# A decoder trunk: eight gate units move into the RG-LRU stage and eight w_rg units into the stick-breaking pairs

## The reference

```
proj = h @ w_in      # RG-LRU x | RG-LRU gelu gate | stick-breaking qkv | FoX qkv | forget logits | 3 merge gates
xa = causal_depthwise_conv(rg_x, conv_w, conv_b)
ya = gelu(rg_gate) * rg_lru(xa, ...)                 # r, i from block-diagonal products, then a scan over tokens
yb = merge_heads(stick_breaking_attention(q_b, k_b, v_b))        # 8 heads x 64
yc = merge_heads(forgetting_attention(q_c, k_c, v_c, log_f))     # 8 heads x 64
g = sigmoid(merge + merge_b).reshape(bsz, slen, 3, 1024)
mixed = g[:, :, 0] * (ya @ w_rg) + g[:, :, 1] * (yb @ w_sb) + g[:, :, 2] * (yc @ w_fox)
return mixed @ w_o
```

## Time and profile before

| what | value |
|---|---|
| median of three runs | 2886.98 us (2884.0 to 2891.76) |
| the profiled execution: its time | 2893.89 us |
| its span, first to last instruction | 2892.1 us |
| PE busy | 2730.0 us (94%), 13124 matmuls |
| DVE, ACT, POOL busy | 1219.5, 1059.9, 1176.4 us |
| mean granted TensorE clock | 0.977 of full speed |

### The profile page before, as it was taken

The page is one execution under the profiler, slowest core; times in us unless marked ns, Lnnn a source line. Parts: engine busy times, 40 slices in busy tenths (PEclk is TensorE's granted clock), DMA queues, the critical chain, the costliest instruction groups (busy, mean ns, idle before and its releaser), DMA issues.

```text
span 2892.1 us, 35341 instructions
## 1 busy us (share of the span) xinstructions
PE 2730.0 (94%) x13124; PEld 2272.7 (79%) x13124; DVE 1219.5 (42%) x1608; ACT 1059.9 (37%) x1593; POOL 1176.4 (41%) x471
## 2 busy tenths in 40 slices
PE   3999998899999999999989999988999999999998
PEld 3888886687788888888888888767777888788886
DVE  6655337855421134511145553577545111444111
ACT  4222236554432234222242222565444322432223
POOL 2555433422234444544435554333221444355443
PEclk9999998999999999999999999989999999999999
DMA  5555531211123333533335555211111333244333
GB/s 213 205 203 190 168 123 59 73 45 44 52 74 96 100 96 111 175 101 102 93 128 200 186 196 160 89 59 53 50 52 44 95 94 96 74 175 142 92 102 95
DMA packets 91303, 325.73 MB, mean 113 GB/s; under 512 B 10097, under 2 KB 12529, under 8 KB 90865
## 3 DMA queue, kind: packets, MB, share of 16 engines
q1 hardware_dynamic: 91120, 323.35, 34.2%
HBM read 321.21 MB, written 2.10 MB: 112 GB/s over the span
## 4 chain that ended last, share of the span: by engine, by line
issue 54%; POOL 33%; PE 12%; POOLq 0%; ACT 0%; DVE 0%; ACTq 0%; DVEq 0%
POOL w_lo L383 32%; PE bank L1143 4%; PE bank L1142 4%; PE bank L1141 4%; POOL wab_lo L389 1%; POOLq L381 0%; ACT fin L729 0%; POOL tmp L366 0%; DVE fin L1134 0%; DVE x L792 0%; ACTq L93 0%; PE bank L1198 0%; ACT rstd L426 0%; ACT tmp L418 0%; ACT rstd L423 0%
## 5 line engine op out<-in xcount | busy, mean ns | idle before, releaser
L383 POOL TENSOR_TENSOR w_lo<-raw,w_hi 128x1024 fp32r<-128x1024 f32 x443 | 1157.5, 2622 | 1565.1 <-ACT w_hi L412 1564.7
L1141 PE MATMUL bank<-h_hi,w_hi 128*128 128x512 f32 x2240 | 883.9, 395 | 0.5
L1142 PE MATMUL bank<-h_lo,w_hi 128*128 128x512 f32 x2240 | 877.8, 392 | 0.0
L1143 PE MATMUL bank<-h_hi,w_lo 128*128 128x512 f32 x2240 | 876.8, 391 | 0.0
L412 ACT ACTIVATE w_hi<-raw 128x1024 fp32r<-128x1024 f32 x443 | 468.1, 1057 | 1010.9 <-PE bank L1143 933.9
L1141 PEld LDWEIGHTS bank<-h_hi,w_hi 128*128 128x128 f32 x2240 | 425.3, 190 | 89.7 <-POOL w_lo L383 1.3
L1143 PEld LDWEIGHTS bank<-h_hi,w_lo 128*128 128x128 f32 x2240 | 424.2, 189 | 89.8
L1142 PEld LDWEIGHTS bank<-h_lo,w_hi 128*128 128x128 f32 x2240 | 425.1, 190 | 87.6
L740 DVE CUSTOM_DVE_ANT_0 ada<-ada,c_act 128x1024 f32<-128x1024 f32 x144 | 255.2, 1779 | 265.3 <-DMA ada<-ada_w 265.1
L1143 PE MATMUL bank<-g_hi,w_lo 128*128 128x512 f32 (+1 forms) x792 | 295.2, 373 | 0.0
L1142 PE MATMUL bank<-g_lo,w_hi 128*128 128x512 f32 (+1 forms) x792 | 292.4, 369 | 0.0
(11 more groups left out here) (200 smaller groups left out, 3055.5 us busy)
## 6 DMA issues: line engine op xcount, KB each, us to landing
raw<-w_units SPq DMA_DIRECT2D x443, 512.0 KB, 3.6
ada<-ada_w SPq DMA_DIRECT2D x144, 512.0 KB, 4.5
ada<-ada_w SPq DMA_DIRECT2D x8, 1024.0 KB, 16.5
x<-x_in SPq DMA_DIRECT2D x4, 512.0 KB, 7.3
wab_raw<-wab SPq DMA_DIRECT2D x2, 1024.0 KB, 5.8
y<-fin SPq DMA_DIRECT2D x8, 256.0 KB, 2.2
c_act<-c_rows SPq DMA_DIRECT2D x1, 512.0 KB, 3.7
vec<-vecs SPq DMA_DIRECT2D x3, 92.5 KB, 3.3
```

Source lines behind the costliest of these rows:

```text
L383: nc.gpsimd.tensor_tensor(w_lo[s][:, :, :], raw[u % RAW][:, :, :], w_hi[s][:, :, :].bitcast(F32), ALU.subtract).then_inc(unit_lo.sem, 1)
L1141: nc.tensor.matmul(o, wh, xh, start=start, stop=False, skip_group_check=True)
L1142: nc.tensor.matmul(o, wh, xl, start=False, stop=False, skip_group_check=True)
L1143: return nc.tensor.matmul(o, wl, xh, start=False, stop=stop, skip_group_check=True)
```

## The change

The first merge gate's eight units (`gate0`, from `h`) now stand in the RG-LRU stage: one in front of each `gates(c)`. Their sigmoids go into a new buffer `part`. The eight w_rg units (`w_rg`, from `ya`) stand in the stick-breaking pairs, two in each: one behind `scores`, one between the next pair's k and v units, both into bank 7. DVE multiplies each into `part` (`first_part`). The merge has three units for each block instead of five and alternates between two sets of banks. The units are numbered and stored in the new order. Because `ya` is used up when the FoX pairs begin, the FoX outputs lie in its memory (`yf_hi`, `yf_lo`), the stick-breaking outputs in `ys_hi`, `ys_lo`; several small buffers of the RG-LRU stage have other addresses. All instructions that compute remain; none is added but in another form (each block's product with the first gate goes into `part` in place of `mx`).

The core of the diff: numbering and memory, then ACT, DVE and PE:

```
+def U_X(c):
+    return U_RG + 6 * (c // 2) + 2 * (c % 2)
+
+
+def U_GATE0(n):
+    return U_RG + 6 * (n // 2) + 4 + n % 2
+
+
+def U_Q(p, j):
+    if p == 0:
+        return U_QKV + j
+    if p <= 4:
+        return U_QKV + 3 + 5 * (p - 1) + (1, 2, 4)[j]
+    return U_QKV + 23 + 3 * (p - 5) + j
+
+
+def U_WRG(n):
+    return U_QKV + 3 + 5 * (n // 2) + (0, 3)[n % 2]
 
 
...
+        yf_hi = at("yf_hi", 0, [P, 4, T], F32R)
+        yf_lo = at("yf_lo", 8192, [P, 4, T], F32R)
+        ys_hi = at("ys_hi", 32768, [P, 4, T], F32R)
+        ys_lo = at("ys_lo", 40960, [P, 4, T], F32R)
+        part = at("part", 49152, [P, KD, T])
+
...
-                tick(l, U_RG + 2 * c0 + 4)
+                tick(l, U_GATE0(c0))
                 nc.scalar.preload_act_table_set("sigmoid_and_others")
                 for c in both:
                     s, b = c % 2, 4 + 2 * (c % 2)
+                    act.wait_ge(unit_done.sem, unit_done.at(l, U_GATE0(c) + 1))
+                    A(part[:, c, :], bank[2 * s + 1][:, :], ACT.Sigmoid,
+                      bias=vec[:, V_MERGEB + c:V_MERGEB + c + 1]).then_inc(sg0_ready.sem, 1)
+                    tick(l, U_GATE0(c) + 1)
...
-                u = U_QKV + 3 * p
+                u = U_Q(p, 0)
+                if 1 <= p <= 4:
+                    tick(l, u - 1)
                 if p:
                     tick(l, u)
...
+            def first_part(l, n):
+
+                if n == 0:
+                    dve.wait_ge(sg0_ready.sem, sg0_ready.at(l, KD))
+                dve.wait_ge(unit_done.sem, unit_done.at(l, U_WRG(n) + 1))
+                V.tensor_tensor(part[:, n, :], part[:, n, :], bank[7][:, :], ALU.mult).then_inc(part_ready.sem, 1)
+
...
+                sg = [tmp[2 * (n % 2) + g] for g in range(2)]
+                dve.wait_ge(sg_ready.sem, sg_ready.at(l, 2 * n + 2))
+                dve.wait_ge(unit_done.sem, unit_done.at(l, U_TAIL + 3 * n + 3))
+                if n == 0:
+                    dve.wait_ge(part_ready.sem, part_ready.at(l, KD))
+                for g in range(2):
+                    V.tensor_tensor(sg[g][:, :], sg[g][:, :], bank[4 + 2 * (n % 2) + g][:, :],
+                                    ALU.mult).then_inc(mx_step.sem, 1)
+                for g in range(2):
+                    dve.wait_ge(mx_step.sem, mx_step.at(l, 4 * n + (1, 3)[g]))
+                    V.tensor_tensor(part[:, n, :], part[:, n, :], sg[g][:, :], ALU.add).then_inc(mx_step.sem, 1)
...
+                for p in range(4):
+                    sb_softplus(l, p, 0)
+                    first_part(l, 2 * p)
+                    sb_softplus(l, p, 1)
+                    q_rest(l, p + 1)
+                    v_rest(l, p)
+                    sb_split(l, p, 0)
+                    sb_split(l, p, 1)
+                    k_rest(l, p + 1)
+                    first_part(l, 2 * p + 1)
+                    y_rest(l, p)
+                for p in range(4, PAIRS):
...
+                    if p < 4:
+                        pe.wait_ge(part_ready.sem, part_ready.at(l, 2 * p + 2))
...
                 pe.wait_ge(vt_ready.sem, vt_ready.at(l, p + 1))
-                if p:
+                if p < 4:
+                    pe.wait_ge(part_ready.sem, part_ready.at(l, 2 * p + 1))
+                else:
...
+            def gate0(l, n):
+                pe.wait_ge(gelu_ready.sem, gelu_ready.at(l, n + 1))
+                unit(l, U_GATE0(n), bank[2 * (n % 2) + 1][:, :], h_hi, h_lo)
+
+            def w_rg(l, n):
+                if n == 0:
+                    pe.wait_ge(yal.sem, yal.at(l, KD))
+                elif n % 2 == 0:
+                    pe.wait_ge(ybl.sem, ybl.at(l, n // 2))
+                else:
+                    pe.wait_ge(vl.sem, vl.at(l, n // 2 + 1))
+                unit(l, U_WRG(n), bank[7][:, :], ya_hi, ya_lo)
 
...
-                gates(l, 0)
-                gates(l, 1)
+                for c in range(2):
+                    gate0(l, c)
+                    gates(l, c)
                 for c in range(2, KD):
                     pe.wait_ge(conv.sem, conv.at(l, 3 * (c - 1)))
-                    unit(l, U_RG + 2 * c, bank[2 * (c % 2)][:, :], h_hi, h_lo)
-                    pe.wait_ge(gelu_ready.sem, gelu_ready.at(l, c - 1))
-                    unit(l, U_RG + 2 * c + 1, bank[2 * (c % 2) + 1][:, :], h_hi, h_lo)
+                    unit(l, U_X(c), bank[2 * (c % 2)][:, :], h_hi, h_lo)
+                    pe.wait_ge(sg0_ready.sem, sg0_ready.at(l, c - 1))
+                    unit(l, U_X(c) + 1, bank[2 * (c % 2) + 1][:, :], h_hi, h_lo)
                     if c % 2:
+                        gate0(l, c - 1)
                         gates(l, c - 1)
+                        gate0(l, c)
                         gates(l, c)
                 qkv(l, 0, 0)
                 qkv(l, 0, 1)
                 qkv(l, 0, 2)
-                for p in range(PAIRS):
+                for p in range(4):
+                    scores(l, p)
+                    w_rg(l, 2 * p)
+                    qkv(l, p + 1, 0)
+                    turn_v(l, p)
+                    suffix(l, p, 0)
+                    suffix(l, p, 1)
+                    qkv(l, p + 1, 1)
+                    w_rg(l, 2 * p + 1)
+                    qkv(l, p + 1, 2)
+                    values(l, p, 0)
+                    values(l, p, 1)
+                for p in range(4, PAIRS):
                     nxt = p + 1 < PAIRS
-                    middle = suffix if p < 4 else turn
                     scores(l, p)
                     turn_v(l, p)
                     if nxt:
...
-                    u = U_MERGE + 5 * n
-                    for g in range(3):
-                        if n:
-                            pe.wait_ge(sg_ready.sem, sg_ready.at(l, 3 * n - 2 + g))
+                    u = U_TAIL + 3 * n
+                    for g in range(2):
+                        if n >= 2:
+                            pe.wait_ge(sg_ready.sem, sg_ready.at(l, 2 * n - 3 + g))
                         if n or g:
-                            unit(l, u + g, bank[g][:, :], h_hi, h_lo)
-                    if n == 0:
-                        pe.wait_ge(yal.sem, yal.at(l, KD))
-                    if n:
-                        pe.wait_ge(mx_step.sem, mx_step.at(l, 5 * n))
-                    unit(l, u + 3, bank[3][:, :], ya_hi, ya_lo)
+                            unit(l, u + g, bank[2 * (n % 2) + g][:, :], h_hi, h_lo)
                     if n == 0:
                         pe.wait_ge(ybl.sem, ybl.at(l, PAIRS))
-                    s = (u + 4) % RING
-                    pe.wait_ge(unit_lo.sem, unit_lo.at(l, u + 5))
+                    if n >= 2:
+                        pe.wait_ge(mx_step.sem, mx_step.at(l, 4 * (n - 2) + 2))
+                    s = (u + 2) % RING
+                    pe.wait_ge(unit_lo.sem, unit_lo.at(l, u + 3))
                     for j in range(KD):
-                        i = mm3(bank[4 + j // 4][:, :], w_hi[s][:, j, :], w_lo[s][:, j, :], yb_hi[:, j, :],
-                                yb_lo[:, j, :], j % 4 == 0, j % 4 == 3)
+                        hi, lo = (ys_hi, ys_lo) if j < 4 else (yf_hi, yf_lo)
+                        i = mm3(bank[4 + 2 * (n % 2) + j // 4][:, :], w_hi[s][:, j, :], w_lo[s][:, j, :],...
```

More of the change, by code:

```diff
@@ L44 @@
 U_RG = FFN_UNITS
-U_QKV = U_RG + 2 * KD
-U_MERGE = U_QKV + 3 * PAIRS
-U_WO = U_MERGE + 5 * KD
+U_QKV = U_RG + 3 * KD
+U_TAIL = U_QKV + 3 * PAIRS + KD
+U_WO = U_TAIL + 3 * KD
 UNITS = 2 * FFN_UNITS + 88
@@ L394, in _ @@
                     lo(l, u)
-                    if U_RG + 3 <= u < U_RG + 3 + 2 * KD and (u - U_RG) % 2 == 1:
-                        wab_lo_part(l, (u - U_RG - 3) // 2)
+                    for c in range(KD):
+                        if u == U_X(c) + 3:
+                            wab_lo_part(l, c)
             for u in range(AHEAD):
@@ L560, in v_copy @@
             def v_copy(l, p):
-                u = U_QKV + 3 * p + 2
+                u = U_Q(p, 2)
+                if 1 <= p <= 4:
+                    tick(l, u - 1)
                 tick(l, u)
@@ L1367, in qkv @@
                     pe.wait_ge((vt_ready, ql, kl)[j].sem, (vt_ready, ql, kl)[j].at(l, p + (0 if j == 0 else 1)))
-                unit(l, U_QKV + 3 * p + j, bank[QKV_BANK(p, j)][:, :], h_hi, h_lo)
+                unit(l, U_Q(p, j), bank[QKV_BANK(p, j)][:, :], h_hi, h_lo)
+            def gate0(l, n):
[9 more added lines that the diff above has]
+                unit(l, U_WRG(n), bank[7][:, :], ya_hi, ya_lo)
             pe.wait_ge(consts_v.sem, 10)
@@ L1402, in _ @@
                     else:
-                        unit(l, U_MERGE, bank[0][:, :], h_hi, h_lo)
-                    middle(l, p, 0)
-                    middle(l, p, 1)
+                        pe.wait_ge(kl.sem, kl.at(l, PAIRS))
+                        unit(l, U_TAIL, bank[0][:, :], h_hi, h_lo)
+                    turn(l, p, 0)
+                    turn(l, p, 1)
                     if nxt:
@@ L1489, in _layout @@
         a = cols(win[:, 0:2 * D])
```

(25 more changed lines are left out.)

142 lines of the change are left out of this document (62 added, 80 removed).

## The result

The changed kernel takes 2812.8 us (median of four runs, 2811.66 to 2819.79) against 2887.08 us before (four runs, 2884.0 to 2891.76). The ratio is 0.9748, with a 95% interval of 0.9732 to 0.9765: 74.3 us less, against 76 forecast. The profiled execution took 2812.3 us, 81.6 less than that of before, which lay 6.8 us over its own median.

What follows compares the result with a forecast made beforehand. PE, busy 94% of the span, bounds the kernel, so only its waits and lower clock can go: 49.7 us in the RG-LRU stage and 26 in the stick-breaking pairs, 2887 − 76 = 2811 us, range 2801 to 2820.

Steps and rivals of the forecast that it cites:

- The price of a unit: On PE at full clock: 5.60 us per w_sb, w_fox or w_rg unit, 5.47 per unit on `h`; merge shrinks 88.6 per layer.
- RG-LRU stage: Added gate units fill PE's waits and lower clock there: 51.7 us lost, 2 left, gain 49.7.
- the correction of the earlier trace for the fall behind `fx_a`: Layer 0, before `gates(2)`: at full clock the 5.06 us wait would have been 1.5 longer, 6.6, leaving about 1.1.
- The term of 51.7 us: Loss of both RG-LRU stretches against 93.3 us each: 34.3 in waits, 17.4 in lower clock and pipeline restart.
- `k_lo`: Wait in front of the first scores: its 7.6 us stay, and the lower clock behind them.
- Stick-breaking pairs: Suffix sums' `e_lo` waits, restarts and clock falls lose 33.0 us; 0.9 a pair, 7 in all, is left; gain 26.
- Restart of 0.25 us: Each `e_lo` wait in the stick-breaking pairs costs PE about 0.25 us beyond its idle time; 15 times, 3.8.
- Rival 1: Clock falls anyway in the stick-breaking pairs, waits perhaps not the cause: 10.4 us do not come, 2821; chance 0.07.
- Rivals 2 and 3: Second: DVE binds the RG-LRU stage, 2826 us, chance 0.07. Third: weights come late to PE, 2928 us, chance 0.03.
- The port rule: DVE and GpSimd share an exclusive lock, loser blocks fully; by it 10 us remain in the pairs, gain 73, not 76.
- my bound of 10: Stick-breaking pairs: 1.3 us times 8 stays if both POOL conversions delay DVE fully; 7 was taken.
- The losses do not depend on the profiler: The 76 us read from the profiled execution (2893.9) were taken off the median of 2887.0 too, giving 2811.

Runs made afterwards that it cites:

- experiment 1: Kernel before, with only the gate units moved into the RG-LRU stage, w_rg left in the merge, first gate's product left out: 2840.22 us.
- experiment 2: Kernel before, with only the w_rg units moved into the stick-breaking pairs, a copy in place of the product, gates left in the merge: 2856.62 us.
- Experiment 6: Changed kernel, with both gate units ahead of both block-diagonal products in the RG-LRU stage: 2817.67 us.
- experiment 5: Changed kernel, with q's and k's first rests ahead of the last scan and the v unit's conversion after both heads' splits: 2797.77 us.
- experiment 3: Changed kernel, with the second weight conversion behind the logarithms (v unit's) moved behind both heads' exponentials in the stick-breaking pairs: 2809.5 us.

## Why the prediction was right, step by step

- **The price of a unit.** A w_rg unit was taken at 5.60, like w_sb: 639.36 to 645.01 is 5.65. The merge of layer 0 shrank by 88.9 us, forecast 88.6.
- **RG-LRU stage.** Full length by the forecast 93.3 + 8 × 5.47 = 137.1 us; measured 137.34 and 137.39. So 0.5 us in all were left where I expected 2: the wait before `gates(2)` is 0.34 us in both layers, not 1.1 and 0.2. So the correction of the earlier trace rows for the fall behind `fx_a` (1.5 us) was too large for layer 0. By the two profiles the gain is 238.3 + 16 × 5.47 − 274.7 = 51.1 us, forecast 49.7; by the medians of experiment 1, 45.1. The term of 51.7 us was the weak one: its 17.4 us for the lower clock and the restarts come from one execution. By experiment 2's profile the same stage loses 227.3 − 2 × 93.3 = 40.7 us: 31.0 in waits, and 9.7 in place of 17.4 for the rest.
- **`k_lo`.** "The 7.6 us for `k_lo` stay": they grew to 8.6. The step holds but for its size. From the end of `gates(7)` to that of `k_lo` it is 20.4 us before and 20.5 after, in both layers. What changed is PE's three units beside it: in layer 0 they took 17.1 us before, partly at the lower clock (0.92 over 18 us), and 16.4 after; in layer 1 16.3 and 16.4. So 0.7 of the 1.0 us is a faster PE that comes to the same wait. Experiment 6 shows that the chain can move too, with what stands before it on ACT.
- **Stick-breaking pairs.** Forecast 0.9 us left per pair, restarts included: measured 0.99 (41.60 against 40.61 of experiment 5). (The prediction's own terms, 0.5 + 0.1 and two restarts of 0.25, add up to 1.1.) The mechanism, POOL's second conversion on the ports that DVE uses, is shown by experiment 3, which moves that conversion alone, and the wait goes. From the stretches: 137.4 + 138.3 + 16 × 5.60 = 365.3 us would be needed with nothing gained, 337.1 were taken, so 28.2 were gained, forecast 26; experiment 2: 28.7.
- **Restart of 0.25 us** for each wait: experiment 5 gives 0.41 / 2 = 0.2.
- **The clock.** Rival 1 (it falls anyway) did not come. With the w_rg units alone in the pairs the clock there is 0.99 and 1.00 (experiment 2); with the waits left as they were it is 0.95 (experiment 1), in the same stage of nearly the same kernel. Layer 1's 0.97 in the changed kernel lies in its first pair, behind the `k_lo` wait: 0.90 over the first 41.6 us, 1.00 in the other three pairs. That the shorter waits bring this, and not the unbroken matmuls of the added units, is argued and not shown. The Trainium skill (TensorE: Matmul & The Clock Gate, the table of what matters for kernels) wants longer gaps for a fall than the 1.0 and 1.5 us here; by that rule 10.4 us would not have come, and the trace does not agree.
- **Rivals 2 and 3.** DVE did not bind the RG-LRU stage in either profile of the changed kernel; one execution of experiment 3 shows a single such wait of 4.68 us, so the mechanism exists and is near. PE never waited for late weights: no `w_lo` is in any list of its waits.
- **The port rule.** By the Trainium skill (SBUF — State Buffer, on the shared port pair) the engine that comes second is blocked until the other's instruction ends. The rows agree: the cast took 2.60 us, where head 0's took 0.56, and `e_lo` 3.03 against 0.96. So both conversions held DVE up, and this cost 0.99 × 8 = 8 us, between my 7 and my bound of 10. The 1.3 us a pair behind that bound is not worked out in the prediction, and no run shows it.
- **The sum against the two times.** "The losses do not depend on the profiler": the profiled executions differ by 81.6 us, the medians by 74.3. The profiled execution of before lay 6.8 us over its own median, and my terms were read from it. For the medians the RG-LRU term was too large (49.7 against 45.1 by experiment 1) and that of the pairs too small (26 against 28.7). These two errors partly cancel. Where each gain comes from is shown; that 76 came so near to 74.3 is partly luck. Of the 81.6 us, 3.1 lie in the two feed-forward blocks between the mixers, where the program is the same: the first gate unit's 5.47 us are new in that span, and it grew by 2.3 only (789.8 to 792.1).

## What to carry to other kernels

Where one engine is busy 94% of the time, add up what a stage would need at full clock from the distances of its instructions' starts and compare it with the stage's length: the difference is what independent work can buy there, waits, restarts and lower clock together. By that measure the RG-LRU stage lost 51.7 us here; with the 33.0 us added up from waits, restarts and falls in the stick-breaking pairs it was 84.7, of which the change took some 75. Take the lost time from more than one execution: in this stage it was 51.7 us in one profile and 40.7 in another. After such a move, look for what else the moved unit brings with it (here its weight conversion on POOL): placing that apart from DVE's critical pieces, and pulling two short rests ahead of a long scan, gave another 15 us.

## What the runs showed of the hardware

- The clock fell four times behind waits of 1.0 and 1.5 us that recur in every one of eight pairs (kernel before), and not once when two waits of 0.5 and 0.1 us and two more units of matmuls stood in their place.
- A FoX pair with the same waits took 29.7 or 31.25 us, according to whether the clock fell in it; two executions of one kernel differed in which pairs those were. This, and who comes first, DVE or POOL, are what the few us between executions consist of where I could follow them.
- A DVE operation of 0.69 us took 2.93 when POOL's conversion began 0.01 us ahead of it, and 0.69 when it began 0.20 us behind.
- Of DVE's busy time a part is waiting: 22.9 against 19.0 us in one pair for the same instructions.
